# The feed-forward output product by one level of Strassen's recursion

## The reference

```python
def conv_gated_ffn(h, w_in, conv_w, conv_b, w_out):      # FFN_DIM = 2816
    a = h @ w_in
    gate, up = a[..., :FFN_DIM], a[..., FFN_DIM:]
    gpad = jnp.pad(gate, ((0, 0), (CONV_WIDTH - 1, 0), (0, 0)))
    conv = conv_b + sum(gpad[:, tap:tap + s] * conv_w[tap] for tap in range(CONV_WIDTH))
    return (jax.nn.silu(conv) * up) @ w_out
...
x = x + conv_gated_ffn(rmsnorm(x, norm_ffn[i]), ffn_w_in[i], ffn_conv_w[i], ffn_conv_b[i], ffn_w_out[i])
x = per_layer_embed(x, p[i], norm_pl[i], pl_w_gate[i], pl_w_proj[i])
```

## Time and profile before

| | |
|---|---|
| median of 3 runs | 1506.84 us |
| the profiled execution: span of its instructions | 1505.3 us |
| TensorE busy, matmuls | 1491.1 us, x6808 |
| VectorE busy | 849.0 us |
| ScalarE busy | 676.1 us |
| GpSimd busy | 795.6 us |
| moved by DMA | 142.14 MB, mean 94 GB/s |

### The profile page before, as it was taken

How to read it: one execution, slowest core, us unless ns; L and a number is a source line. 1 busy time by engine, 2 the same in 40 slices (tenths; PEclk the granted TensorE clock), 3 DMA queues, 4 the chain that set the end, 5 groups by cost and what they waited for, 6 DMA issues and landing times.

```text
span 1505.3 us, 19989 instructions
## 1 busy us (share of the span) xinstructions
PE 1491.1 (99%) x6808; PEld 1234.9 (82%) x6808; DVE 849.0 (56%) x1294; ACT 676.1 (45%) x1019; POOL 795.6 (53%) x980
## 2 busy tenths in 40 slices
PE   9999999999999999999999999999999999999997
PEld 6888888888888888888888888888788888888886
DVE  7998996455555411159874655646755555511145
ACT  6887886433323322237563543635633333322243
POOL 5343344666666755457345253551566666655452
PEclk9999999999999999999999999999999999999999
DMA  4121111322222322242132322320222222332221
GB/s 178 57 71 56 42 56 63 106 98 98 98 98 98 133 103 97 73 168 99 56 143 102 107 89 85 133 99 33 94 104 91 98 97 98 118 111 97 93 80 60
DMA packets 42838, 142.14 MB, mean 94 GB/s; under 512 B 4256, under 2 KB 10528, under 8 KB 42784
## 3 DMA queue, kind: packets, MB, share of 16 engines
q1 hardware_dynamic: 41248, 138.82, 26.3%
q10 hardware_dynamic: 1536, 2.61, 0.5%
HBM read 139.32 MB, written 2.10 MB: 94 GB/s over the span
## 4 chain that ended last, share of the span: by engine, by line
PE 96%; DVE 2%; ACT 1%; DMA 1%; issue 0%; POOL 0%; SPq 0%; POOLq 0%; DVEq 0%; ACTq 0%
PE bank L602 26%; PE bank L605 26%; PE bank L606 26%; PE bank L880 3%; PE bank L885 3%; PE bank L884 3%; PE bank L680 2%; PE bank L660 1%; PE bank L661 1%; PE bank L691 1%; PE bank L690 1%; DMA x<-in_xT 1%; PE bank L1033 0%; DVE sumsq L1122 0%; PE bank L663 0%
## 5 line engine op out<-in xcount | busy, mean ns | idle before, releaser
L548 POOL TENSOR_TENSOR wl<-raw,wh 128x256 fp32r<-128x256 f32 x752 | 616.1, 852 | 476.4 <-ACT wh L1708 476.4
L602 PE MATMUL bank<-xh,wh 128*128 128x512 f32 (+1 forms) x1160 | 451.4, 389 | 1.0 <-DVE xl L1128 0.8
L606 PE MATMUL bank<-xh,wl 128*128 128x512 f32 (+1 forms) x1160 | 450.2, 388 | 0.0
L1708 ACT ACTIVATE wh<-raw 128x1024 fp32r<-128x1024 f32 (+1 forms) x212 | 235.0, 1108 | 478.8 <-PE bank L602 388.7
L605 PE MATMUL bank<-xl,wh 128*128 128x512 f32 (+1 forms) x1160 | 450.0, 388 | 0.0
L602 PEld LDWEIGHTS bank<-xh,wh 128*128 128x128 f32 x1160 | 217.8, 188 | 47.2 <-DVE xl L1128 2.1
L606 PEld LDWEIGHTS bank<-xh,wl 128*128 128x128 f32 x1160 | 217.9, 188 | 44.7
L605 PEld LDWEIGHTS bank<-xl,wh 128*128 128x128 f32 x1160 | 217.8, 188 | 43.8
L564 POOL TENSOR_TENSOR wl<-raw,wh 128x256 fp32r<-128x256 f32 x160 | 127.2, 827 | 194.4 <-ACT wh L1708 194.4
L1148 DVE TENSOR_TENSOR x<-x,bank 128x512 f32<-128x512 f32 x56 | 38.5, 688 | 254.0 <-PE bank L606 254.0
L602 PE MATMUL bank<-yh,wh 128*128 128x512 f32 x352 | 136.9, 389 | 0.0
(11 more groups left out here) (224 smaller groups left out, 2332.4 us busy)
## 6 DMA issues: line engine op xcount, KB each, us to landing
raw<-in_w SPq DMA_DIRECT2D x180, 512.0 KB, 3.2
raw<-in_w SPq DMA_DIRECT2D x32, 704.0 KB, 4.0
rc<-in_w SPq DMA_DIRECT2D x16, 512.0 KB, 3.8
w_end<-in_w SPq DMA_DIRECT2D x8, 512.0 KB, 4.1
rb<-in_w SPq DMA_DIRECT2D x8, 512.0 KB, 5.9
x<-in_xT SPq DMA_DIRECT2D x4, 512.0 KB, 7.5
pin<-in_pT ACTq DMA_DIRECT2D x2, 512.0 KB, 3.1
rotary<-in_consts ACTq DMA_DIRECT2D x1, 512.0 KB, 3.5
```

Of the source, the lines that this page charges most:

```text
L548: last = nc.gpsimd.tensor_tensor(wl[:, slot, cols], part[:, cols], wh[:, slot, cols].bitcast(F32), ALU.subtract)
L602: first = mm(out, ah_, bh_, start=start, stop=False, skip_group_check=True)
L606: return mm(out, al_, bh_, start=False, stop=stop, skip_group_check=True)
L1708: nc.scalar.activation(out, in_, ACT.Copy, bias=0.0, scale=scale).then_inc(done, 1)
```

## The change

The output product becomes Strassen's. w_out is cut in four: A11, A12, A21, A22 of 4 output chunks by 11 blocks (output chunks 0 to 3 and 4 to 7; even and odd f), and y into Y11, Y12 (even f, early and late 256 tokens), Y21, Y22 (odd f). Seven products of 11 blocks by 256 tokens take the place of eight, each with four output chunks, so 28 *pieces* of 33 matmuls of 256 columns. Four of the seven have sums of weight quarters on the left (S1 to S4), and the right-hand sides are sums too (T1 to T4). In `PIECES` the pieces stand in order, in `LOADS` the loads:

```diff
+PIECES = ([("A11", m) for m in range(K2)]
+          + [(kind, m) for m in range(K2) for kind in ("S1", "S3")]
+          + [("S2", 0), ("S2", 1), ("A22", 0), ("S2", 2), ("A22", 1), ("S2", 3), ("A22", 2), ("A22", 3)]
+          + [("S4", 0), ("S4", 1), ("S4", 2), ("A12", 0), ("S4", 3), ("A12", 1), ("A12", 2), ("A12", 3)])
+POOL_BLOCKS = 8
+LOADS = ([("A11", 0, "s0"), ("A11", 1, "r0"), ("A11", 2, "r1"), ("A21", 0, "r0"), ("A22", 0, "r1"),
+          ("A11", 3, "s3"), ("A11", 1, "s1"), ("A11", 2, "s2"), ("A21", 1, "r0"), ("A22", 1, "r3"),
+          ("A22 again", 2, "r2"), ("A21", 2, "r0"), ("A22", 2, "r1"), ("A21", 3, "r0"), ("A22", 3, "r3")]
+         + [("A22 again", 0, "r0"), ("A22 again", 1, "r1"), ("A22 again", 3, "r3")]
+         + [("A12", m, f"r{m}") for m in range(K2)])
...
+            zh, zl = sb("zh", [FH, HALF], F32R, ph), sb("zl", [FH, HALF], F32R, ph)
+                s3 = sb("s3", [FH * P], F32, before_s3)
         xh, xl = sb("xh", [KC, T], F32R), sb("xl", [KC, T], F32R)
```

SyncE's waits ahead of the loads:

```diff
+                    if (what, m) == ("A11", 0):
+                        sp_eng.wait_ge(w_low, end - 2)
+                    elif what == "A11" and into[0] == "r":
+                        sp_eng.wait_ge(w_low, end - 2 + m)
+                    elif (what, m) == ("A21", 0):
+                        piece_low(PIECE["A11", 1])
+                    elif (what, m) == ("A22", 0):
+                        piece_low(PIECE["A11", 2])
+                    elif into == "s3":
+                        sp_eng.wait_ge(f_begun, f_count(layer, 0))
...
+                    elif what == "A21":
+                        sums_made(m - 1)
```

GpSimd makes the low parts of the first eight blocks of each piece, VectorE those of the last three (`low_part`):

```diff
+                for q in range(N_PIECES):
+                    held = [blocked(part[:, piece_slot(layer, q), :]) for part in (wh, wl)]
+                    pool.wait_ge(f_high, f_count(layer, q))
+                    for b in range(0, POOL_BLOCKS, LOW_BLOCKS):
+                        part = slice(b, b + LOW_BLOCKS)
+                        last = nc.gpsimd.tensor_tensor(held[1][:, part, :], piece_source(q)[:, part, :],
+                                                       held[0][:, part, :].bitcast(F32), ALU.subtract)
+                    last.then_inc(f_low_p, 1)
```

TensorE, a piece:

```diff
+                for q, (kind, m) in enumerate(PIECES):
+                    out = bank[m if kind in ("S1", "S4") else K2 + m][:, 0:HALF]
+                    opens = kind in ("A11", "S1", "A12")
+                    pe.wait_ge(f_low_p, f_count(layer, q))
+                    pe.wait_ge(f_low_v, f_count(layer, q))
...
+                    elif kind == "S1":
+                        pe.wait_ge(chunk_freed, C_PL[layer] - K2 + m + 1)
+                    else:
+                        before = {"S3": "A11", "S2": "S3", "A22": "S2", "S4": "S1", "A12": "A22"}[kind]
+                        pe.wait_ge(f_freed, f_count(layer, PIECE[before, m]))
+                        pe.wait_ge(right_low, 5 * layer + ready[kind])
...
+                        last = three(out, *blk(piece_slot(layer, q), k), high[:, k, :], low_[:, k, :], opens and k == 0,
+                                     k == FH - 1, begins=k == 0, begun=f_begun)
+                    last.then_inc(f_prod, 1)
```

VectorE's order in `out_stage` (`take` adds a finished bank, or subtracts it, to the quarters of x that it belongs to; sum1 to sum4 are one instruction of 1408 columns each; right_lows is the low part of a right-hand side, one instruction of 2816; t4 another):

```diff
+                beside = {
+                    0: lambda: sum1(0),
+                    1: lambda: (right_lows(1, zl, Y11, zh, 1), sum3(0)),
+                    3: lambda: (sum1(1), sum3(1)),
+                    5: lambda: (sum1(2), sum3(2)),
+                    6: lambda: (right_lows(2, xa_l, Y12, xa_h, -1), t4()),
+                    7: lambda: (sum1(3), sum3(3)),
+                    9: lambda: (sum2(0), sum2(1)),
+                    11: lambda: sum2(2),
+                    12: lambda: right_lows(3, ya_l, Y12, ya_h, -1),
+                    13: lambda: sum2(3),
+                    15: lambda: norm_open(norm),
+                    16: lambda: (sum4(0), x_lows(0)),
+                    17: lambda: (squares(0), sum4(1)),
+                    18: lambda: (right_lows(4, xa_l, Y22, xa_h, 1), x_lows(1)),
+                    19: lambda: (sum4(2), squares(1)),
+                    20: lambda: (sum4(3), x_lows(2)),
+                    21: lambda: (right_lows(5, ya_l, Y21, ya_h, 1), squares(2)),
+                    22: lambda: (x_lows(3), squares(3)),
+                    24: p_lows,
...
+                for q in range(2):
+                    low_part(q)
+                for j in range(N_PIECES + 1):
+                    if j:
+                        take(j - 1)
+                    if j + 2 < N_PIECES:
+                        low_part(j + 2)
+                    if j in beside:
+                        beside[j]()
```

More of the change, by code:

```diff
@@ L1353, in ffn @@
                                                      ALU.add).then_inc(conv_step, 1)
+                        if u:
+                            dve.wait_ge(t1_high, FH * layer + i + 1)
+                            low(one(ya_l, i), one(y, f - 1)[:, late], one(ya_h, i), t1_low)
                         dve.wait_ge(chunk_done, c + 2)
@@ L1721, in tile_high @@
                     return
+                for layer in range(2):
+                    if N_PL[layer] <= like < N_PL[layer] + RING:
+                        q, free = N_PIECES - RING + like - N_PL[layer], 0
+                        if q == N_PIECES - 1:
+                            act.wait_ge(f_prod, f_count(layer, q))
+                        else:
+                            act.wait_ge(f_begun, f_count(layer, q + 1))
                 if free:
@@ L1880, in ffn, with turn @@
                 nc.scalar.preload_act_table(ACT.Silu)
-                def turn(i, like, step):
+                def turn(i, ahead):
                     for u in range(2):
@@ L1886, in turn @@
                         at = layer * FC + f
-                        tile_high(like + RING + 2 * u, i, step)
+                        ahead(2 * u)
+                        if u:
+                            act.wait_ge(t1_full, FH * layer + i + 1)
+                            copy(one(ya_h, i), one(y, f - 1)[:, late], t1_high)
                         act.wait_ge(conv_step, CONV * at + CONV)
                         nc.scalar.activation(conv[:, u, :], conv[:, u, :], ACT.Silu).then_inc(gate_silu, 1)
-                        tile_high(like + RING + 2 * u + 1, i, step)
@@ L1891, in turn @@
[L1891 to L1892 removed]
+                        ahead(2 * u + 1)
+                        if u == 0:
+                            act.wait_ge(y_full, at + 1)
+                            copy(one(xa_h, i), one(y, f)[:, early], y11_high)
                 with act.Fori(0, last) as i:
[L1894 to L1896 removed]
@@ L1897, in ffn @@
-                act.dma_start(pin[:], pT[layer]).then_inc(p_loaded, 16)
-                act.wait_ge(p_loaded, 16 * (layer + 1))
-                for q in range(PC):
-                    copy(pinh[:, q, :], pin[:, q, :], p_high)
-                n0, last = N_FFNOUT[layer], KC // 2 - 1
-                def out_turn(i, like, step):
-                    for u in range(2):
-                        tile_high(like + RING + 2 * u, i, step)
-                        tile_high(like + RING + 2 * u + 1, i, step)
-                        x_chunk(C_FFNOUT[layer] + 2 * i + u, norm + 1, 2 * i + u, u % 2)
@@ new lines, in ffn @@
+                right_highs(1, zh, Y11, 1.0)
+                piece_high(layer, RING - 1)
+                for j in range(1, N_PIECES - RING + 1):
+                    if j in (18, 20):
+                        beside[j]()
+                    piece_high(layer, j + RING - 1)
+                    if j in beside and j not in (18, 20):
+                        beside[j]()
+                for t in range(RING):
+                    tile_high(N_PL[layer] + t)
+                    if t:
+                        x_chunk_beside(K2 + t)
```

332 lines of the change are left out of this document (263 added, 69 removed).

## The result

The changed kernel takes **1550.68 us** (median of four, 1549.31 to 1551.87) against 1506.82 before: a ratio of 1.029, 95% interval 1.0276 to 1.0306. It is slower by 43.9 us, where the prediction said 38 (1545 us), with a range from 1518 to 1566. The profiled execution has a span of 1550.0 us, 44.7 above that of before.

A forecast was written before the change was run, and what follows sets the result against it. TensorE bounds the kernel before; after, the port shared by VectorE and GpSimd: 12.0 + 58.4 + 48.5 + 19.8 = 138.7 us a stage against 119.7, 38 in all on 1506.8, so 1545 us, range 1518 to 1566.

The forecast's parts named there:

- TensorE's share: Output product: 924 matmuls of 256 columns, 3.95 us a piece, 110.7 a layer, 8.9 less than before.
- The port: Output stages: VectorE instructions with two SBUF operands and GpSimd's exclude each other, so a piece comes every 5.1 us.
- start until GpSimd begins piece 3: Stage beginning: the third load lands at 10.5 us, ScalarE's copy takes 1.4, GpSimd begins piece 3 at 12.0.
- VectorE's holds: Time VectorE's two-SBUF-operand instructions keep GpSimd off the shared port, up to the low of piece 23: 48.5 us a layer.
- the five pieces after: Stage end, after the low of piece 23: GpSimd gets ahead and TensorE runs at its own pace, 19.8 us.
- the port doesn't decide: Rival: VectorE's work falls in GpSimd's idle time or overlaps; stage 114 to 120 us, 1496 to 1508; chances 0.08 faster, 0.04 unchanged.
- the signs by which the prediction said that it would be wrong: Mid-stage GpSimd gaps, its instructions near 0.8 us, longest waits ended by DMA or VectorE's `wl`, clock well under 1.00.
- TensorE waits for it nearly all the way: Output stage: GpSimd's low part comes every 5.1 us where TensorE needs 3.95, so TensorE waits at nearly every piece.
- GpSimd's share of a pair: GpSimd's time in an alternating VectorE-GpSimd pair: 0.61 us, at most 0.695; bound given as -6 to +2 a layer.
- The lock over a long instruction: VectorE's right-hand lows of 2816 columns hold the shared ports throughout, blocking GpSimd 2.9 us each.
- The clock: Rival: waits of 3 to 5 us slow TensorE's clock, +4 to +12 us a layer, 1553 to 1569; chance 0.15.
- The start: Stage beginning: piece 0 waits for VectorE's low_part(0), behind the last f; TensorE idles some 3.3 us.

The follow-up runs named there:

- the kernel with the waits removed: Changed kernel with VectorE's operand from a bank, early low parts and A21 loaded once, its output not the product: 1502.1 us, ratio 0.9967 to before.

## Why the prediction was right, and where it was off

**TensorE's share**: as worked out. 0.120 us a matmul of 256 columns, 3.96 a piece; the layer would be 110.7, and the kernel with the waits removed comes to 114.8 with 3.5 us of waits. The gain of 8.9 us a layer is there and is the smaller part; the waits cost about three times that.

**The port**: right in kind (28 of 43.9 us came back with the operand in a bank), nearly right in size. Take the first stage by the prediction's own terms, up to the low part of piece 23, which ends at 635.64 + 4.02 = 639.66, 121.7 us after 518.0:

- start until GpSimd begins piece 3: 12.9 (predicted 12.0). The three s loads were issued from 522.67 on; s3 is the first of them. It landed 6.7 us after its issue, and ScalarE began its copy at 529.45, 1.4 us before GpSimd began. Layer 1: 13.0.
- 21 pieces of GpSimd's own work: 58.4, as predicted.
- VectorE's holds: 48.5 were predicted. GpSimd is in its 21 pieces for 121.7 - 12.9 - 6.9 = 101.9, so the holds, what is left over the 58.4, are 43.5. In layer 1, 120.9 - 13.0 - 6.1 = 101.8. Some sums (545.29 is one) fell where GpSimd idled and held nobody.
- GpSimd's own gaps: 3.87 + 3.04 = 6.9; layer 1 3.04 + 3.04 = 6.1. Predicted: none.
- the five pieces after: 21.4 in layer 0 and 19.9 in layer 1 (predicted 19.8). The 1.6 of layer 0 are the clock: at 639.66 TensorE was still in S4,2, which ran from 636 to 639.4 by steps of 0.21:

```profile
637.48 0.41 PE L736 MATMUL psum<-xa_h,wl 128*128 128x256 f32 x1
637.69 0.41 PE L732 MATMUL psum<-xa_h,wh 128*128 128x256 f32 x1
```

12.9 + 58.4 + 43.5 + 6.9 + 21.4 = 143.1. The step that failed is the sentence "From 12.0 GpSimd has never a gap, as ScalarE makes the highs faster than 2.78". ScalarE does, but it has to have a sum first, and the sum a load. The prediction looked at how fast each producer is, and not at what a tile waits for before it is loaded: r0 is read by sum3(0), which ends at 537.04; SyncE issues A21,1 at 537.11 and A22,1 at 537.48, and their sum begins at 545.29, 7.8 us on, as A22,1 lands 7.7 us after its issue (A21,1 took 4.3). Only then come the high and GpSimd at 548.46. The rival "the port doesn't decide" had this cost at 0 to 6 a layer, and it is of that size. The forecast left it out, and in the first third of the stage GpSimd had no work in hand to cover it. That the total came out so close is in part luck: two errors of the first stage, -5.0 and +6.9, nearly cancel. Over both layers the stages are 6.5 us longer than forecast: 2.9 from these two, 1.9 from the start, 1.7 from the end.

Of the signs by which the prediction said that it would be wrong, two are there: GpSimd has gaps in the stage, and the clock reads 0.95. The others are not: GpSimd's instructions do not stay near 0.8, and TensorE's longest waits end with GpSimd's low part. "TensorE waits for it nearly all the way", at S1 and S3 above all, is not what the trace shows either. The waits are 26.1 us of the first stage (27.9 a layer was said), but in bunches, with 7.3 of them at S1 and S3 and 9.8 at S2 and S4. A mean of 5.1 us a piece gave the sum of the waits and not their places.

One of the bounds was worked out wrongly. With 0.55 instead of 0.61 as GpSimd's share of a pair, the prediction's own rule gives 51 x 0.06 = 3 us less, 135.6 and not 133. With 0.695 it gives 4 more and not 2. The range does not hang on it. The work on y in the first product was costed at 0.7 us more of VectorE for each pair of f. It is 2.2: ten chunks, five pairs, go from 56.5 to 67.7 us. The stretch is no longer for it, so that cost was rightly put at nothing.

**The lock over a long instruction**: no row of before showed 2816 columns. Now one instruction of GpSimd's takes 3.58 us beside `zl<-y,zh`. It starts at 531.98, after `zl` (531.33), and ends at 535.56, 0.6 us after `zl` does (534.97), which is nearly its time alone (0.695). The Trainium skill (SBUF — State Buffer, Who interferes with whom) has the two engines' shared ports as a lock that is held for the whole instruction, and the trace agrees. It agrees too where an operand comes from a bank: there GpSimd's four instructions beside `zl` took 3.21 us and not 7.79.

**The clock**: the prediction's rival said +4 to +12 a layer. The fall was real (0.95 over each stage, seven stretches at 1.2 GHz over the two, after waits of 2 to 5 us) and cost nothing that could be measured (1.6 us in one layer by the account above). Its condition was wrong: it is not enough that a slow piece (5.5 to 6.2 us here) is longer than the 5.1 that the port needs on the mean; it must be so where no later wait of TensorE takes the loss up. The slow piece 3 of layer 0 had the next operand there in time (GpSimd was done at 541.8, piece 3 at 545.0), but the wait before piece 8 took it up. Only behind S4,2 in layer 0 did no wait follow.

**The start**: predicted 3.3, measured 3.4, and worth 5.2 us in all when taken away. **The wait before piece 3**: about 4 was said, 5.4 and 4.0 measured. **Length near 139, GpSimd near 120, its mean near 1.2**: 143 and 141, 122, 1.01 to 1.33.

## What to carry to other kernels

Here 8.9 us of matmuls a layer were bought with 84 us more on VectorE and 61 more on GpSimd, holds counted in. Before such a trade, add GpSimd's time and VectorE's with two SBUF operands as if they were one engine's, and compare the sum with TensorE's new time. Then follow every buffer once round (load, sum, high, low, next load), since a mean rate hides a loop whose one turn is longer than a piece. A slow clock after a wait cost time here only where no further wait came behind it in the stage.

## What the runs showed of the hardware

- A broadcast bank operand in place of a second SBUF operand, same columns, brought a GpSimd instruction of 256 columns from 1.33 us to 0.84 on the mean of 52: to free the port it was enough to move one operand.
- 256-column matmuls with waits of 2 to 5 us among them lost the 2.4 GHz level for short stretches; some 150 matmuls of 256 columns a layer on constants, in eight of those waits, kept the granted clock at 0.99 to 1.00 over the stage.
- Five loads of 704 KB issued within 2.2 us (521.82 to 523.95) landed 3.9, 5.3, 6.7, 7.9 and 10.2 us after their issue, where one alone takes 4.0. A load of the same size into y, in rows of 128 elements, took 4.9 and 4.7 us where it went alone (611.24 and 616.18).
